# A hybrid decoder step on Trainium2: two products of the recurrence's last head move from GpSimd to VectorE, and two weight blocks of the projection behind it are fetched earlier

## What is computed

```python
def rglru_layer(h, conv_buf, h0, w_in, conv_w, conv_b, w_a, b_a, w_x, b_x, lam, w_out):
    xb, gate = jnp.split(h @ w_in, 2, axis=-1)
    y = conv_b + sum(xpad[:, j:j + s] * conv_w[j] for j in range(C_CONV))
    r = jax.nn.sigmoid(jnp.einsum('bsnd,nde->bsne', yh, w_a).reshape(b, s, C_WIDTH) + b_a)
    i = jax.nn.sigmoid(jnp.einsum('bsnd,nde->bsne', yh, w_x).reshape(b, s, C_WIDTH) + b_x)
    log_a = -C_GATE_C * r.astype(jnp.float32) * jax.nn.softplus(-lam.astype(jnp.float32))
    a = jnp.exp(log_a)
    u = jnp.sqrt(-jnp.expm1(2.0 * log_a)) * (i * y).astype(jnp.float32)
    ...
    _, hs = lax.associative_scan(lru_combine, (a, u), axis=1)
    out = (hs.astype(h.dtype) * jax.nn.silu(gate)) @ w_out
```

## Time and profile before

| | us |
|---|---|
| median of three runs | 2446.91 |
| lowest and highest run | 2445.93, 2453.77 |
| the profiled execution, time | 2443.1 |
| the profiled execution, span from first to last instruction | 2441.3 |

### The profile page before, as it was taken

The page is one execution under the profiler, slowest core; times in us unless marked ns, Lnnn a source line. Parts: engine busy times, 40 slices in busy tenths (PEclk is TensorE's granted clock), DMA queues, the critical chain, the costliest instruction groups (busy, mean ns, idle before and its releaser), DMA issues. The chain is left out here.

```text
span 2441.3 us, 47634 instructions
## 1 busy us (share of the span) xinstructions
PE 2292.1 (94%) x17886; PEld 1901.0 (78%) x17886; DVE 1252.1 (51%) x1972; ACT 1097.7 (45%) x1873; POOL 722.9 (30%) x809
## 2 busy tenths in 40 slices
PE   7989999999889999999968989989899999999998
PEld 6956666666688999999968989989896566666668
DVE  5133555566443666766674166681412355655552
ACT  4055544555344544455552256661302655545541
POOL 2134322333030222332233325541211532322311
PEclk9999999999999999999979999999999999999999
DMA  4020434434331111111102111101213023434333
GB/s 151 26 75 1 122 107 114 112 95 120 121 130 45 49 51 55 40 50 54 46 28 106 35 53 49 40 20 52 70 35 117 28 83 108 119 102 112 110 105 139
DMA packets 104278, 187.62 MB, mean 77 GB/s; under 512 B 15722, under 2 KB 84332, under 8 KB 102916
## 3 DMA queue, kind: packets, MB, share of 16 engines
q1 hardware_dynamic: 104068, 184.81, 24.6%
HBM read 164.84 MB, written 19.92 MB: 76 GB/s over the span
## 5 line engine op out<-in xcount | busy, mean ns | idle before, releaser
L1507 POOL TENSOR_TENSOR latents_t_lo<-pages_t,latents_t_hi 128x256 fp32r<-128x256 f32 x256 | 187.7, 733 | 551.4 <-ACT latents_t_hi L1744 550.7
L1906 DVE TENSOR_REDUCE sums<-w_uq 128x8 f32<-128x512 f32 x256 | 175.2, 684 | 263.1 <-ACT w_uq L1752 262.8
L1752 ACT ACTIVATE w_uq<-ps 128x512 f32<-128x512 f32 x256 | 152.8, 597 | 209.6 <-PE ps L1592 208.8
L2209 PE MATMUL ps<-src_hi,w_hi 128*128 128x344 f32 x720 | 243.3, 338 | 2.8 <-ACT normed L2365 2.6
L1592 PE MATMUL ps<-w_uk_hi,latents_t_hi 128*128 128x512 f32 x512 | 236.1, 461 | 1.0 <-POOL latents_t_lo L1507 1.0
L2209 PE MATMUL ps<-src_hi,w_lo 128*128 128x344 f32 x720 | 233.5, 324 | 0.0
L2209 PE MATMUL ps<-src_lo,w_hi 128*128 128x344 f32 x720 | 233.4, 324 | 0.0
L1592 PE MATMUL ps<-w_uk_lo,latents_t_hi 128*128 128x512 f32 x512 | 203.7, 398 | 0.0
L1592 PE MATMUL ps<-w_uk_hi,latents_t_lo 128*128 128x512 f32 x512 | 203.3, 397 | 0.0
L1761 ACT ACTIVATE latents<-ps,bias,rq 128x256 f32<-128x256 f32 (+7 forms) x128 | 106.1, 829 | 131.3 <-DVE bias L1920 117.5
L1606 PE MATMUL ps<-residual,normed 96*128 96x512 f32 (+3 forms) x384 | 153.6, 509 | 8.8 <-ACT w_uq L1752 6.2
(11 more groups left out here) (368 smaller groups left out, 5582.3 us busy)
## 6 DMA issues: line engine op xcount, KB each, us to landing
pages_t<-in_pages_t SPq DMA_DIRECT2D x256, 208.0 KB, 2.6
pages<-in_pages SPq DMA_DIRECT2D x256, 128.0 KB, 2.1
w_slots<-in_w_hgrn SPq DMA_DIRECT2D x30, 512.0 KB, 3.6
w_slots<-in_w_mla_in SPq DMA_DIRECT2D x18, 512.0 KB, 3.7
x_home<-residual SPq DMA_DIRECT2D x2, 4128.0 KB, 14.5
w_slots<-in_w_rg SPq DMA_DIRECT2D x14, 512.0 KB, 3.5
residual<-in_x SPq DMA_DIRECT2D x8, 516.0 KB, 9.0
residual<-in_x SPq DMA_DIRECT2D x1, 4128.0 KB, 13.8
```

Of the source, the lines that this page charges most:

```text
L1507: nc.gpsimd.tensor_tensor(lat_lo[:, g % DEPTH, :, :].rearrange("p k t -> p (k t)"), ring[:, g % RING, 0:KVL], lat_hi[:, g % DEPTH, :, :].r ...
L1752: nc.scalar.activation(sq[:, g % 2, :], keys(g), ACT.Square).then_inc(squared, 1)
L1906: nc.vector.tensor_reduce(ss[:, b % 2, p, :], sq[:, g % 2, :].rearrange("p (h d) -> p h d", h=H), AX.X, ALU.add).then_inc(ssum, 1)
L2209: mm = nc.tensor.matmul(bank[:, 0:TT], w[:, slot, kk, :], x[:, kk, cols], start=(kk == 0 and m == 0), stop=(kk == KD - 1 and m == 2))
```

## The change

Three things change, all around the last head.

1. In the last head GpSimd no longer makes `gated` for head 6 and `iy` for head 7. VectorE makes both: `gated(h - 1, 1 - u)` ahead of the first `out_hi`, and `iy` behind `out_lo(1)`.
2. SP fetches `w_out[2]` and `w_out[3]` at the end of the heads' stage, as soon as the low parts of `w_out[0]` and `w_out[1]` are made and the slots are free; it waits for both at the end of its list. The next stage then neither fetches them nor makes ScalarE wait for them (`ring.loaded`).
3. In the next stage the low part of block 2 is made by VectorE, between its additions of blocks 0 and 1. GpSimd starts with that of block 3.

```diff
@@ streamed_projection
+        loaded = ring is not None and ring.loaded
...
-            elif ring is not None:
+            elif ring is not None and not loaded:
                 for u in range(2):
                     sp.dma_start(ws[:, u, :, :], w[2 + u]).then_inc(w_landed[u], 16)
...
             def weight_hi(m, u, landed):
-                act.wait_ge(w_landed[u], landed)
+                if not loaded or not isinstance(m, int) or m > 3:
+                    act.wait_ge(w_landed[u], landed - (16 if loaded else 0))
                 wait(act, summed, m - 1)
...
-            for m in range(ready, 4):
+            if loaded:
+                pool.wait_ge(w_lo_done, 1)
+            for m in range(3 if loaded else ready, 4):
                 weight_lo(m, m % 2)
...
+            if loaded:
+                one(0, 0)
+                dve.wait_ge(w_hi_done, 1)
+                nc.vector.tensor_tensor(w_lo[:, 0, :, :], ws[:, 0, :, :], w_hi[:, 0, :, :].bitcast(F32),
+                                        ALU.subtract).then_inc(w_lo_done, 1)
+                one(1, 1)
             if x_in is None:
-                with dve.Fori(0, pairs - (1 if norm else 0)) as i:
+                with dve.Fori(1 if loaded else 0, pairs - (1 if norm else 0)) as i:
@@ rglru_heads, SP
+            for n in range(2):
+                sp.wait_ge(w_lo_done, 2 * H + (n + 1))
+                sp.dma_start(ws[:, n, :, :], w_out[2 + n]).then_inc(w_more, 16)
+            ring.loaded = True
             sp.wait_ge(kept_conv, 3 * H)
...
             ring.stores = 4
+            sp.wait_ge(w_more, 32)
@@ rglru_heads, GpSimd
                 weight_lo(following if following is not None else H, 1)
+                if following is None:
+                    return
...
-                if following is None:
-                    return
@@ rglru_heads, VectorE
+            def gated(h, u):
+                dve.wait_ge(h_done, 3 * h + 3)
+                dve.wait_ge(gs_done, h + 1)
+                nc.vector.tensor_tensor(out[:, h, :], hs[:, :], graw[:, u, :], ALU.mult).then_inc(og_done, 1)
...
                 if following is None:
+                    gated(h - 1, 1 - u)
                     for kk in range(BY_DVE):
                         out_hi(kk)
                         out_lo(kk)
+                    dve.wait_ge(i_done, h + 1)
+                    nc.vector.tensor_tensor(iy[:, :], iy[:, :], y[:, u, :], ALU.mult).then_inc(iy_done, 1)
...
                     out_lo(5)
-                    dve.wait_ge(gs_done, h + 1)
-                    nc.vector.tensor_tensor(out[:, h, :], hs[:, :], graw[:, u, :], ALU.mult).then_inc(og_done, 1)
+                    gated(h, u)
```

More of the change, by code:

```diff
@@ L220, in __init__ @@
         self.stores = 0
+        self.loaded = False
     def piece(self, c, m, k, t):
@@ L2745, in rglru_heads @@
         wg_landed = [st.sem("wg_landed0"), st.sem("wg_landed1")]
+        w_more = st.sem("w_more_landed")
         w_hi_done = st.sem("w_hi_done")
```

## The result

| | before | changed |
|---|---|---|
| median of 22 runs each, us | 2452.27 | 2442.84 |
| lowest and highest, us | 2444.38, 2460.43 | 2432.80, 2449.28 |
| span of the profiled execution, us | 2441.3 | 2447.4 |

The ratio of changed to before is 0.9958, 95% interval 0.9946 to 0.9971: faster by 7 to 13 us. Two disturbed executions are left out of the ratios of this document, one of experiment e2 (7082.92 us) and one of before on the chip of e10 to e12 (2613.23 us). The profiled execution of the changed kernel is nevertheless 6.1 us *longer* than that of before. So the two spans can't be compared; the places must be.

The account below looks back on a forecast made before the run. TensorE, busy 94% of the span, was taken as the bound, so only its waits and clock could pay. Gains 3.1 + 2.85 + 2.9 = 8.85 us gave 2438.1 against the median, full range 2433.5 to 2443.0.

Parts of the forecast that it names:

- Step 1: Last head, two products moved from GpSimd to VectorE: TensorE starts the pieces at 1629.93 instead of 1633.03, gaining 3.1 us.
- A: Place where the last head's pieces start; as measured stretch, from its gate matmuls to the projection stage's table load.
- R1: Rival: VectorE's stalls in the last head are not GpSimd's; total gain 4.6 us, time 2442.3; chance 0.08.
- The clock at A: Start of the last head's pieces: clock still falls, costing the same 2.5 us; term 0, bounds −0.4 and +1.2.
- R3: Rival: the clock doesn't fall at the start of the last head's pieces; total gain 10.15 us, 2436.8; chance 0.06.
- R4: Slower rival: clock stays at 1.2 GHz through all the last head's pieces; +8.4 us, 2455.3; chance 0.03.
- Steps 2 and 3: Projection stage, early weight transfers and VectorE's low part: TensorE starts block 2 at 1659.95 instead of 1662.80, gaining 2.85 us.
- The clock at B: Block 2 of the projection stage: with TensorE's wait cut to 1.15 us the clock stays at 2.4 GHz, gaining 2.9 us.
- B: Place where projection block 2 starts; as measured stretch, from that stage's table load to the next stage's table load.
- The sum: Total gain at the last head's pieces and projection block 2: 3.1 + 2.85 + 2.9 = 8.85 us.
- forecast case: Both places behave as predicted: gain 6.9 to 10.0 us, time 2436.9 to 2440.0; chance 0.66.
- R2: Rival: the clock isn't won at projection block 2, or falls longer at the pieces; total 5.95 us, 2441.0; chance 0.17.

Follow-up runs that it names:

- e2: Changed kernel with both products back on GpSimd, keeping early weight transfers and block 2's low part on VectorE; ratio to before 0.9983 (0.9961 to 1.0005).
- e10: Only the two products moved to VectorE against before, plus three unread matmuls behind the pieces; ratio to before 0.9984 (0.9959 to 1.0008).
- e12: The changed kernel run again, nothing altered; ratio to before on the same chip 0.9943 (0.9922 to 0.9963), median 2440.61 us.
- e5: Changed kernel with one product, i*y, back on GpSimd; stretch A 33.27 us against 30.83 in the changed kernel; no whole-time ratio.
- e3: Changed kernel with block 2's low part back on GpSimd; TensorE's wait at block 2 is 2.16 us, B 76.90 us; no ratio.
- e4: Changed kernel with weights 2 and 3 fetched late again; TensorE's wait at block 2 is 2.75 us, B 77.50 us; no ratio.
- e1: Only the two products moved to VectorE against before, weights fetched late as before; ratio to before 1.0027 (1.0004 to 1.0050).

## Why the prediction was right

- **Step 1, 3.1 us.** Measured 3.10 (A 33.93 to 30.83). The wait of TensorE is 4.43 us for 4.4, the root step starts at 1642.28 for the 1632.8 forecast plus 9.48, root·iy stands where it was. e5 and e2 show that the stalls were GpSimd's, so R1 falls. The rule that the forecast puts beside step 1 speaks of VectorE instructions with two inputs. The low part has two, the 128x8 copy has one: for the copy the runs speak, not that rule.
- **The clock at A, 0 within −0.4 and +1.2.** 5.28 us slow instead of 5.29. R3 and R4 did not occur. In the six traces with the same work at A it varied by 0.3 us (30.54 to 30.83), by 15 to 18 slow matmuls; with other lists it was 10 to 21.
- **Steps 2 and 3, 2.85 us.** Block 2 starts 4.11 us behind the stage's start for 4.23 forecast, a gain of 2.97. Split, each half is as forecast in its wait (e3, e4).
- **The clock at B, 2.9 us.** 5.73 − 2.97 = 2.76 us. I called half of it luck of the record. It wasn't: B with the long wait was 80.00, 79.84, 79.79 and 79.59 in four traces, and with the short one 74.25 to 74.27 in six.
- **The sum, 8.85 us.** Measured 8.83 in the two traces, 9.4 between the medians of 22 runs, 7 to 13 by the interval. That 8.85 and 8.83 agree to 0.02 is luck: A and B of one kernel differ by some tenths of a us between traces.
- **The predicted time.** Predicted 2438.1, measured 2442.84. The base was off: the median of before over 22 runs is 2452.27 and not the 2446.91 of three, which lay 7.8 us apart and not 7. These 5.4 us, less the 0.6 by which the gain of the medians is larger, are the 4.7 between forecast and result. The range of the forecast case, 2436.9 to 2440.0, was missed. The measured time lies in the full range, by 0.16 us, only because that was widened for the spread and for R1 and R2, which didn't occur.
- **What I hadn't in the sum.** I took work away from the places as staying as it was. Elsewhere the trace of the changed kernel is 15 us longer (span +6.1 with −8.8 in A and B). For this change, over 22 runs, that evens out within the interval. For step 1 alone it didn't: 3 us less were expected of it, and both its ratios came out above 1.

Two things are left open: whether step 1 alone is really slower as a kernel, or no different (its two intervals leave 1.0004 to 1.0027 in common), and what decides which length an attention stage takes.

## What to carry to other kernels

Look for a stall of VectorE that ends with a GpSimd instruction: moving a 2.4 us product from GpSimd to VectorE cost 1.15 us there and took away a stall of about 2 us, so the busier engine became free earlier. A wait of TensorE costs more than its length once the clock falls behind it, so shortening one from 4.0 to 1.05 us paid 5.7 us, nearly half of it by the clock. At A, where the clock fell behind 7.53 us and behind 4.43, shortening paid only its 3.1 us. Where executions of one kernel differ by more than the change is worth, compare stretches of the trace between fixed instructions, and check in the whole time that what was gained isn't given back in a stage that the change doesn't touch.

## What the runs showed of the hardware that wasn't expected

- The granted clock fell behind a TensorE wait of 2.16 us in the midst of solid work (e3: 0.76 over the next 7.2 us), and held behind 1.05 us (1.00, changed kernel).
- In the fourteen traces the two attention stages took 428.0 to 428.2, 434.4 to 434.6 or 440.1 to 440.2 us (first) and 428.6 to 429.5, 434.5 or 440.0 us (last), with the same instructions. In the three whole stages of before, the changed kernel and e1 TensorE idles for 12.7 to 12.9 us and the granted clock is 0.99, 0.98 and 0.96. Outside A and B the traces differ by 15.8 us, and the sum of the two attention stages by 17.2 us: most of the spread between executions is there. The other stages together differ by 7 us.
- The 0.47 us of extra matmuls of e10 went with a ratio of 0.9984 against 1.0027 and 1.0011 without them, nominally 6.6 to 10.5 us *less*, though the intervals overlap.
